# Expert stage of a two-layer encoder trunk: where VectorE builds the next expert's one-hot matrices

## What is computed

```python
logits = (t @ w_router).astype(jnp.float32) + b_router.astype(jnp.float32)
top_vals, top_idx = lax.top_k(logits, TOP_K)                 # TOP_K = 2 of 8
weights = jax.nn.softmax(top_vals, axis=-1)
combine = jnp.sum(jax.nn.one_hot(top_idx, N_EXPERTS) * weights[..., None], axis=1)
for e in range(N_EXPERTS):
    out = out + combine[:, e:e + 1] * swiglu(t, w_up[e], w_down[e])
# swiglu: gate, up = split(h @ w_up); (silu(gate) * up) @ w_down
# w_up[e] is 1024 x 7168, w_down[e] 3584 x 1024, both float32
```

## Time and profile before

| | us |
|---|---|
| median of 3 runs | 1881.16 (1880.9 to 1881.74) |
| span of the profiled execution | 1878.5 |
| TensorE matmul busy in it | 1657.3 (88%) |
| VectorE busy | 1489.8 (79%) |
| ScalarE busy | 1044.7 (56%) |
| DMA | 498.48 MB, 265 GB/s over the span |

### The profile page before, as it was taken

One profiled execution on the slowest core, in us unless ns is written; L12 is line 12 of the kernel. 1 busy time (PEld: TensorE's weight loads), 2 busy tenths in 40 slices (PEclk: granted clock), 3 DMA queues, 4 the chain that ended last, 5 costly groups with the idle time before them and its releaser, 6 DMA issues.

```text
span 1878.5 us, 22572 instructions
## 1 busy us (share of the span) xinstructions
PE 1657.3 (88%) x7672; PEld 1338.6 (71%) x7672; DVE 1489.8 (79%) x1580; ACT 1044.7 (56%) x1010; POOL 272.2 (14%) x167
## 2 busy tenths in 40 slices
PE   1777776999869897859999999999999999999995
PEld 0766665777657775647778878878788788787883
DVE  5377956688696776678889889799798898897986
ACT  0442223444334443337777777777777776776773
POOL 0348264213232222400000000000000000000000
PEclk9997877999889998969999999999999999999997
DMA  8451332687664555439999999999999999999992
GB/s 275 149 179 46 115 132 90 222 286 270 230 224 144 185 188 215 164 118 316 375 313 346 363 332 363 349 332 381 315 348 363 332 357 354 332 376 335 332 357 109
DMA packets 347594, 498.48 MB, mean 265 GB/s; under 512 B 8504, under 2 KB 271952, under 8 KB 347536
## 3 DMA queue, kind: packets, MB, share of 16 engines
q1 hardware_dynamic: 343888, 489.90, 76.2%
q0 software_dynamic: 1856, 6.01, 1.1%
q10 hardware_dynamic: 1792, 1.83, 0.3%
HBM read 496.66 MB, written 1.05 MB: 265 GB/s over the span
## 4 chain that ended last, share of the span: by engine, by line
PE 66%; DVE 8%; issue 8%; POOL 3%; ACT 1%; DVEq 0%; POOLq 0%; ACTq 0%
PE bank L706 20%; PE bank L708 20%; PE bank L707 20%; DVE acc L1517 3%; PE bank L1098 2%; PE bank L1111 1%; POOL w_part L2137 1%; PE bank L1118 1%; DVE arena L2063 1%; DVE hs L1597 1%; DVE w_part L1557 1%; PE bank L702 0%; DVE small L1603 0%; ACT w_part L1231 0%; POOL mod L2151 0%
## 5 line engine op out<-in xcount | busy, mean ns | idle before, releaser
L1568 DVE TENSOR_TENSOR w_lo<-ring,w_hi 128x2048 fp32r<-128x2048 f32 x338 | 772.1, 2292 | 130.9 <-ACT w_hi L1437 124.4
L1437 ACT ACTIVATE w_hi<-ring 128x2048 fp32r<-128x2048 f32 x336 | 641.4, 1915 | 142.2 <-PE bank L708 132.2
L706 PE MATMUL bank<-w_lo,heT_hi 128*128 128x512 f32 x896 | 359.4, 401 | 2.0 <-issue 1.8
L708 PE MATMUL bank<-w_hi,heT_hi 128*128 128x512 f32 x896 | 350.5, 391 | 0.0
L707 PE MATMUL bank<-w_hi,heT_lo 128*128 128x512 f32 x896 | 349.8, 390 | 0.0
L1231 ACT ACTIVATE w_part<-ring 128x1024 fp32r<-128x1024 f32 (+1 forms) x162 | 168.9, 1049 | 272.6 <-PE bank L708 254.7
L1557 DVE TENSOR_TENSOR w_part<-ring,w_part 128x1024 fp32r<-128x1024 f32 (+1 forms) x105 | 128.7, 1248 | 162.8 <-ACT w_part L1231 162.8
L706 PE MATMUL bank<-w_part,hT_hi 128*128 128x512 f32 (+1 forms) x448 | 181.3, 405 | 24.5 <-POOL w_part L2137 16.7
L2137 POOL TENSOR_TENSOR w_part<-ring,w_part 128x1024 fp32r<-128x1024 f32 (+1 forms) x57 | 139.6, 2454 | 418.5 <-ACT w_part L1231 395.5
L706 PEld LDWEIGHTS bank<-w_lo,heT_hi 128*128 128x128 f32 x896 | 168.3, 188 | 35.8 <-DVE w_lo L1568 2.2
L708 PEld LDWEIGHTS bank<-w_hi,heT_hi 128*128 128x128 f32 x896 | 168.2, 188 | 35.7
(11 more groups left out here) (340 smaller groups left out, 2046.8 us busy)
## 6 DMA issues: line engine op xcount, KB each, us to landing
ring<-in_moe_w_up SPq DMA_DIRECT2D x226, 1024.0 KB, 7.6
ring<-in_moe_w_down SPq DMA_DIRECT2D x112, 1024.0 KB, 6.9
ring<-in_cond_w SPq DMA_DIRECT2D x24, 2048.0 KB, 8.6
ring<-in_ffn_w_up SPq DMA_DIRECT2D x22, 1024.0 KB, 7.7
ring<-in_od_w_in SPq DMA_DIRECT2D x8, 2048.0 KB, 7.8
ring<-in_ev_w_in SPq DMA_DIRECT2D x5, 2048.0 KB, 7.6
ring<-in_ffn_w_down SPq DMA_DIRECT2D x5, 2048.0 KB, 7.6
ring<-in_od_w_in SPq DMA_DIRECT2D x8, 1024.0 KB, 6.5
```

What stands on the lines that cost most here:

```text
L706: mm(bank, lhs[0], rhs[1], start=start, stop=False)
L708: return mm(bank, lhs[0], rhs[0], start=False, stop=stop)
L1437: f(w_hi[:, (n + 2 * late) % 3], w[:, half * PIECE:(half + 1) * PIECE], ACT.Copy) \
L1568: tt(w_lo[:, buf], at, w_hi[:, buf].bitcast(F32), ALU.subtract).then_inc(S["w_lo"], 1)
```

## The change

VectorE's `build()` moves from round 0 of an expert (after `add_back`) to round 14, behind `eT_lo` of the last up unit. Its wait for the bank in which TensorE transposes the old `pw_tok` goes with it, and the base for its step counter. Nothing is added or removed.

```diff
                     if u == 0:
                         add_back(it)
-
-                        item_filled(dve, it, "pwT")
-                        V.n, V.base = 0, it * BUILD_STEPS + steps_before
-                        build()
                     if 1 <= u <= N_UP:
                         dve.wait_ge(S["act_hi"], it * N_UP + u)
                         bank, free = item_filled(dve, it, "act_T", u - 1)
                         to = slice(2 * u - 2, 2 * u)
                         tt(eT_lo[:, to], bank[:, 0:256].rearrange("p (j s) -> p j s", j=2),
                            eT_hi[:, to].bitcast(F32), ALU.subtract).then_inc(free, 1)
+                    if u == N_UP:
+
+                        item_filled(dve, it, "pwT")
+                        V.n, V.base = 0, it * BUILD_STEPS + steps_before
+                        build()
```

## The result

| | before | changed |
|---|---|---|
| median of 6 runs | 1880.75 us | 1888.51 us |
| lowest to highest | 1879.65 to 1881.74 | 1886.84 to 1895.99 |
| ratio | | **1.0047** (95% interval 1.0034 to 1.0061) |
| span of the profiled execution | 1878.5 us | 1887.2 us |
| first `back` to last `back` in it | 1013.0 us | 1020.6 us |

The change makes the kernel slower by 0.47%: 8.8 us by the ratio, 7.8 by the two medians. The profiled executions differ by 8.7 us, of which 7.6 lie in the expert loop (1863.12 - 842.50 against 1853.52 - 840.51) and the rest outside it; the parts outside the loop are the same program and vary from execution to execution. So from here on the loop of the traces is the measure, and the timed runs stand beside it.

What follows compares the result with a forecast made beforehand. TensorE was taken as the bound but for a 1.32 us wait per expert, with loads close behind. Seven experts at +0.86 us and the first at +1.08 gave +7.1 us on 1881.16: 1888.3 us, range 1885 to 1891.5.

Steps and rivals of the forecast that it cites:

- The wait that goes: Transposes of unit 0: TensorE's wait for VectorE's e_a vanishes, giving back at most 1.32 us per expert, 10.6 in all.
- What is left of it: Last up transposes: only 0.22 us of the 1.32 arrives, in the first expert nothing.
- The pinned station: ScalarE's copy starting when the fourteenth up unit's load arrives: stays 68.76 us after `back`, however early TensorE is.
- the two steps taken from the first expert: End of up projection: transposes 7.24 us after the load-bound copy starts, the next ones 5.75 us later.
- all of it passes: Rival: loads speed up when asked for earlier; -0.24 us per expert, 1879.2 us, counted as the same; chance 0.12.
- The new wait: At the gather: TensorE waits 1.08 us in every expert for the moved build; being early does not shorten it.
- S: Start of an expert's last up transposes, from which the prediction counts the build's end and the gather.
- The sum: From `back` to gather: +0.86 us in experts two to eight, +1.08 in the first, together +7.1 us.
- The spread of the forecast: Whole kernel: 0.1 to 0.6 us of the old wait kept per expert, 1885 to 1889.5 us; chance 0.55.
- Nothing is queued behind: After the moved build: later rests of pieces 32 and 33 and later `tokens_lo` cost nothing.
- the build would be hidden: Rival: VectorE finishes the build before TensorE reaches the gather and all 1.32 us passes; 1870.6 us; chance 0.03.
- none of the gain would be left: Rival: only the last up unit's load counts, the 0.22 us goes too; 1889.8 to 1890.5 us; chance 0.27.

Runs made afterwards that it cites:

- e9_seven_parts_and_pwt: Build cut in seven parts in rounds 4 to 10, ScalarE's pwT copy moved to round 1; 125.15 us per expert, ratio 0.9938 to the kernel before.
- e4_half_loads_after: Changed kernel, each up unit loading only 512 of its 1024 rows; 127.21 us per expert, ratio 1.0011 to the kernel before.
- e8_after_pwt_later: Changed kernel with ScalarE's copy of the transposed pwT moved from round 0 to round 1; 126.28 us per expert, ratio 0.9974 to the kernel before.
- e7_signal_early: Changed kernel, p_ready raised after the two p_tok instructions, before the two for pw_tok; 127.10 us per expert, ratio 1.0011 to the kernel before.
- e1_late_gather: Changed kernel with TensorE's gather one down unit later, its uses one round later; 127.14 us per expert, ratio 1.0018 to the kernel before.

## Why the prediction was right

1. **The wait that goes.** Right in its mechanism: `e_a` starts with the SiLU's end, and the transposes of unit 0 come 6.61 us after `back` instead of 7.90. Its price was read as idle time, 1.32 us per expert and 10.6 in all. Counted between starts the wait was 7.90 - 6.42 = 1.48 us: the change gave back 1.29 of it, and e9_seven_parts_and_pwt all of it, with a loop 11.9 us shorter.
2. **What is left of it.** Forecast 0.22 us at the last transposes; measured 81.97 - 81.65 = 0.32. The pinned station, forecast at 68.76 us after `back`, came at 68.66, although the unit was asked for 0.60 us earlier; from there the two steps taken from the first expert came as 1302.48 - 1295.24 = 7.24 and 1308.23 - 1302.48 = 5.75, to the hundredth. e4_half_loads_after and e8_after_pwt_later show the mechanism: without the full queue, or with the sixth unit issued earlier, the lead stays. By the rule of the Trainium skill ("Perfetto Trace Analysis", Roofline), a practical ceiling of about 120% of 358 GB/s for a single core, the loads had room. The trace does not agree in the up projection, where the rows are 1 KB: 350 GB/s at a share of 1.10 in both kernels, against 409 and 410 at 1.03 in the down projection with its rows of 4 KB. That the length of the rows makes the difference was not tried.
3. **A taker that was not named.** The prediction let the front gain stand at 1.32 us until the last up unit. In truth TensorE waits 0.32 us (of idle time) already at piece 4, whose rest was where it had been. The sum came out by luck at this step: it did not notice, since the loads would have taken as much anyway. But the rival "all of it passes" was thus priced wrongly: with loads out of the way the changed kernel is still 0.57 us per expert behind (e4), not 0.24 ahead.
4. **The new wait.** Forecast S + 6.78, measured S + 6.77. e7_signal_early shows that it shrinks by 0.51 us when 0.52 us of the build are taken off it.
5. **The sum.** Experts two to eight were forecast at 0.86 us more from `back` to gather; the measured ones are 0.75 in the fourth, and 0.11 more in the gather itself: 0.86 for the whole expert. In this expert two misses of a tenth cancel, by luck. Over experts two to eight the gather comes 0.74 to 1.06 us later, 0.85 in the mean, and the 0.11 comes on top: 0.96 each. The first expert was forecast at +1.08 and came at 128.58 - 127.67 = +0.91. So the loop is 7.6 us longer where 7.1 were forecast, and the term that was left out is the slower gather. 1888.3 us were forecast and 1888.51 measured; that they lie 0.2 apart is luck too, since the six runs of the changed kernel lie 9 us apart. The spread of the forecast reaches to 1889.5 in the prediction, but 8 x 1.08 less 0.1 per expert gives 1889.0.
6. **"Nothing is queued behind."** True only behind the wait itself. e1_late_gather shows that the rest of piece 32 becomes late as soon as the gather does not stand in front of its matmuls.

The rivals: that the build would be hidden fell (6.77 us after the last transposes in every expert). That none of the gain would be left (1889.8 to 1890.5) lies within what the runs allow; the traces decide against it, with 0.32 us of the lead left at the last transposes of the fourth expert (0.01 in the second, 0.18 to 0.33 in the others behind it).

## What to carry to other kernels

Before a block of work is moved on an in-order engine, count at the new place from the last event of the other engine on which both sides hang: there the block waited for S + 4.7 while its reader came at S + 5.7, and no lead won elsewhere could change that. A gain at the front of a loop is worth what the tightest later station lets through, here a copy on a third engine and then a load queue that a full ring had pinned; moving ScalarE's copy alone was worth nothing, cutting the build in seven alone 0.16 us per expert, and both together 1.48 us. And 2 us of work that fit at none of three places in one piece (rounds 0, 8 and 14) fit in rounds 4 to 10 in pieces smaller than the room of the next thing in line.

## What had not been expected of the hardware

- A wait costs a little more than its idle time in the profile. The transposes of unit 0 lost a wait of 1.32 us and moved by 7.90 - 6.42 = 1.48. A matmul's record is 0.39 us long while the next starts 0.23 later, so 0.16 of a wait lies under the last record before it. Likewise 0.92 us of idle time before the gather stand for 6.77 - 5.70 = 1.07. A loss under 0.16 us at each piece does not show as idle time at all: in the first expert of the kernel before, TensorE's rounds late in the up projection last 5.94 to 6.07 us, the pace of the loads, instead of 5.69, and no idle time stands beside them.
- The gather's 32 matmuls take 3.59 us until the next piece starts when TensorE has waited for them (1318.59 - 1315.00), and 3.48 when it has not (1312.76 - 1309.28 before the change). Eight times 0.11 us is 0.9 of the 7.6. All of it lies between the starts of the first two matmuls, 0.21 us apart after the wait and 0.11 without it; the other distances are the same. Why it is so was not tried.
- The part of the kernel outside the loop, the same in all these kernels, moves the time by more than most of the edits did: the kernel before ran from 1873.17 to 1887.93 us in 31 runs on one chip, while experts three to seven took 126.63 us each in its trace. In the traces of all thirteen kernels the part outside the loop takes from 859.4 to 872.8 us.
